# A top-k search and a projection share one stage: four units of projection move from beside the second search to behind it

## The reference, cut to what matters

```
h = rms_norm(x, norm_g[layer])
proj = h @ w_in[layer]
q, k, v, qi, ki, wi, z_a, u_b, z_b, gates = jnp.split(proj, SPLIT_POINTS, axis=-1)
...
logits = jnp.einsum('bqhd,bsd->bqhs', qib, ki)
iscore = jnp.einsum('bqhs,bqh->bqs', jax.nn.relu(logits), wib).astype(jnp.float32)
iscore = jnp.where(allowed[None], iscore, -jnp.inf)
_, idx = lax.top_k(iscore, k_sel)
...
a = dsa_attention(q, k, v, qi, ki, wi, k_sel) * jax.nn.silu(z_a)
b = multiscale_pool(u_b, pool_w[layer], pool_scale[layer]) * jax.nn.silu(z_b)
g = jax.nn.sigmoid(gates.reshape(B, S, N_BRANCHES, D_MODEL) + merge_bias[layer])
```

## Time and profile before

| | |
|---|---|
| median of 3 runs | 3318.81 us (3316.91 to 3326.31) |
| profiled execution | 3323.57 us, span of its trace 3321.8 us |
| TensorE busy | 3110.3 us (94%) |
| DVE, ACT, POOL busy | 1732.5, 1552.3, 956.3 us |
| second search (32 tries) | 808 to 988 us of the span |
| masks of the second batch, then the barrier | 988 to 1042 us of the span |

### The profile page before, as it was taken

The page is one execution under the profiler, slowest core; times in us unless marked ns, Lnnn a source line. Parts: engine busy times, 40 slices in busy tenths (PEclk is TensorE's granted clock), DMA queues, the critical chain, the costliest instruction groups (busy, mean ns, idle before and its releaser), DMA issues. The chain is left out here.

```text
span 3321.8 us, 43017 instructions
## 1 busy us (share of the span) xinstructions
PE 3110.3 (94%) x15772; PEld 2529.6 (76%) x15772; DVE 1732.5 (52%) x3657; ACT 1552.3 (47%) x2448; POOL 956.3 (29%) x701
## 2 busy tenths in 40 slices
PE   8995999889995999997999799979999999989998
PEld 7994888768884677765778678868888888868787
DVE  6775799989996665536531166642211231133423
ACT  4544688756983677762111143324444354431111
POOL 3541012200222566642222133312322222212222
PEclk9996999999997999998999899989999999999999
DMA  5656333253334621106552345464344543355422
GB/s 177 206 182 231 96 96 100 80 189 110 100 102 155 198 78 51 39 20 192 155 146 93 131 150 161 140 212 142 114 131 137 197 125 118 119 152 157 133 102 89
DMA packets 431706, 440.63 MB, mean 133 GB/s; under 512 B 31008, under 2 KB 324256, under 8 KB 431392
## 3 DMA queue, kind: packets, MB, share of 16 engines
q1 hardware_dynamic: 431520, 438.18, 42.7%
HBM read 279.51 MB, written 158.60 MB: 132 GB/s over the span
## 5 line engine op out<-in xcount | busy, mean ns | idle before, releaser
L1342 PE MATMUL p_pr<-p_hT,p_w_hi 128*128 128x512 f32 x896 | 354.8, 396 | 16.1 <-POOL p_w_lo L1095 10.0
L1343 PE MATMUL p_pr<-p_hT,p_w_hi 128*128 128x512 f32 x896 | 352.3, 393 | 0.0
L1344 PE MATMUL p_pr<-p_hT,p_w_lo 128*128 128x512 f32 x896 | 352.0, 393 | 0.0
L1628 POOL TENSOR_TENSOR a_prob<-a_prob,a_inv 128x1024 f32<-128x1024 f32 (+12 forms) x104 | 250.7, 2419 | 211.2 <-DVE a_inv L1673 211.0
L1135 ACT ACTIVATE p_relu<-p_isc,p_level 128x2048 int8<-128x2048 f32 (+5 forms) x192 | 276.4, 1441 | 22.5 <-DVE p_level L1232 17.7
L791 PE MATMUL t_pj_ps<-t_w_hi,t_hT_slot 128*128 128x356 f32 (+2 forms) x768 | 272.2, 354 | 11.5 <-DVE t_w_lo L639 5.9
L1095 POOL TENSOR_TENSOR p_w_lo<-p_w_raw,p_w_hi 128x256 fp32r<-128x256 f32 x144 | 107.5, 777 | 603.7 <-DVE p_level L1232 399.6
L793 PE MATMUL t_pj_ps<-t_w_hi,t_hT_slot 128*128 128x356 f32 (+2 forms) x768 | 265.2, 345 | 0.0
L792 PE MATMUL t_pj_ps<-t_w_lo,t_hT_slot 128*128 128x356 f32 (+2 forms) x768 | 264.8, 345 | 0.0
L1648 DVE CUSTOM_DVE_ANT_0 a_prob<-a_s_ps,a_mask 128x512 f32<-128x512 f32 (+3 forms) x320 | 189.4, 607 | 141.2 <-PE a_s_ps L1782 136.5
L2260 PE MATMUL o_b_ps<-o_in_hi,o_w_hi 128*128 128x512 f32 x512 | 209.0, 408 | 39.5 <-DVE o_in_lo L2147 27.4
(11 more groups left out here) (291 smaller groups left out, 7120.4 us busy)
## 6 DMA issues: line engine op xcount, KB each, us to landing
s_hT<-t_hT_slot SPq DMA_DIRECT2D x32, 1024.0 KB, 5.9
s_gT<-p_o_sb SPq DMA_DIRECT2D x128, 256.0 KB, 4.9
o_gates<-s_gT SPq DMA_DIRECT2D x64, 512.0 KB, 5.1
p_w_raw<-in_w_in SPq DMA_DIRECT2D x56, 512.0 KB, 4.3
t2n_w_raw<-in_w_in SPq DMA_DIRECT2D x56, 512.0 KB, 4.2
s_qT<-t_qT_slot SPq DMA_DIRECT2D x32, 512.0 KB, 2.7
p_hT<-s_hT SPq DMA_DIRECT2D x32, 512.0 KB, 9.3
s_zuT<-p_o_sb SPq DMA_DIRECT2D x64, 256.0 KB, 4.8
```

The source lines that it names most:

```text
L1342: nc.tensor.matmul(pr[n % NPR][:], wh, hi, start=(k == 0), stop=False)
L1343: nc.tensor.matmul(pr[n % NPR][:], wh, lo, start=False, stop=False)
L1344: last = nc.tensor.matmul(pr[n % NPR][:], wl, hi, start=False, stop=(k == KD - 1))
L1628: nc.gpsimd.tensor_tensor(p, p, f, ALU.mult).then_inc(normed, 1)
```

## The change

`TRY_UNITS[1]` ends at 102 in place of 106. So thirty units, 72 to 101, stand beside the 32 tries of the second search in place of thirty-four, and ten, 102 to 111, behind it in place of six. Only seven `sides` and mask stores stand there, so the two loops of SP and ACT now run on behind the seventh.

```diff
     IDX_UNITS = [(0, 15), (52, 72)]
-    TRY_UNITS = [(15, 52), (72, 106)]
+    TRY_UNITS = [(15, 52), (72, 102)]
...
             last = TRY_UNITS[1][1]
-            for b in range(-2, NB):
-                if b >= 0:
+            for b in range(-2, N_UNITS - last):
+                if 0 <= b < NB:
                     store_mask(1, b)
                 if last + b + 2 < N_UNITS:
                     unit(last + b + 2)
...
-            for b in range(NB):
-                sides(1, b)
-                if b < N_UNITS - TRY_UNITS[1][1]:
-                    unit(TRY_UNITS[1][1] + b)
+            for b in range(N_UNITS - TRY_UNITS[1][1]):
+                if b < NB:
+                    sides(1, b)
+                unit(TRY_UNITS[1][1] + b)
```

## The result

| | before | after |
|---|---|---|
| median of 8 runs | 3322.23 us (3316.91 to 3328.23) | 3332.18 us (3325.77 to 3336.07) |
| profiled execution, its span | 3323.57, 3321.8 us | 3336.07, 3334.3 us |

The ratio is 1.0029, 95% interval 1.0018 to 1.0040: 9.6 us slower, 6 to 13 us by the interval. The two profiled executions are 12.5 us apart, and this stage accounts for most of that. It is measured from DVE's first count of the second search to the next stage's first load, since the search began 0.93 us later in the new trace: 1042.23 - 808.57 = 233.66 us before, and 1053.78 - 809.50 = 244.28 us after, 10.6 us more.

What follows compares the result with a forecast made beforehand. DVE's chain was taken to set the search and masks to end the stage; after the change TensorE's late last units end it, next load at 1053.8 against 1042.23: +11.6 us on 3318.81 gives 3330.4 us, range 3323 to 3336.

Steps and rivals of the forecast that it cites:

- search, to the last level: Second search on DVE: no try has two units, so the store wait at try 15 goes, -2.5 us.
- settling: DVE's small steps behind the search's last level, carried over unchanged at 7.4 us.
- fifth signs: ACT's signs behind the search, waiting for DVE's third mask to be combined; due at 1016.2.
- rest of chunk 55: POOL's w_lo of the last chunk, beside DVE's fourth mask: begun at 1018.7, ready at 1024.6.
- unit 108: TensorE behind the search: starts at 1024.6 after 7 us idle, takes 7.76 us at a low clock.
- last evacuation to the next stage's first load: Stage end: store issued near 1049.5, landing 3.0 us, then 1.25 us to the next load at 1053.8.
- the split of chunk 55: On ACT behind the search: the deciding step, now behind signs that wait for the third mask.
- POOL's blocks: w_lo parts beside the masks: one meeting a DVE scan or combination ends about 0.6 us after it.
- The price for DVE: Masks behind the search: an estimated 1.2 us for each that meets POOL, one before, three now.
- TensorE's lag in the search: TensorE waits 1.9 us for chunk 46's w_lo, growing to 2.9 us by chunk 52; costs the stage nothing.
- the stall ahead of 106: TensorE behind the search waits for chunk 53's w_lo, from 993.8 to 1004.2, then a low clock.
- SP: Chunk 55's load delays unit stores, so ACT's evacuation of unit 104 waits until 1010.2 at most; cost 0.

Runs made afterwards that it cites:

- e2: Twelve units behind the second search in place of the six of the kernel before: stage 258.09 us, median 3345.89 us, ratio 1.0075.
- e3: Changed kernel, but ACT splits chunk 55 behind unit 104's evacuation, ahead of the fourth signs: stage 235.59 us, median 3323.49 us, ratio to before 1.0008.
- e1: Eight units behind the second search in place of the six of the kernel before: stage 232.99 us, median 3321.52 us, ratio 1.0006.
- e4: Changed kernel, but DVE in place of POOL forms w_lo of chunks 53, 54 and 55: stage 238.42 us, median 3325.30 us, ratio to before 1.0017.
- e6: Kernel before, but one unit per try and three in the last try of the second search: stage 229.75 us, median 3316.88 us, ratio 0.9988.
- e5: e1 with the stores of units 110 and 111 issued ahead of the seventh mask's store: stage 231.11 us, median 3317.31 us, ratio to before 0.9988.

## Why the prediction held

Times are from the first count of the search, so that both traces can be compared.

| step | predicted | found |
|---|---|---|
| search, to the last level | 179.4 - 2.5 = 176.9 | 176.8 |
| settling | 7.4, as before | 6.0 |
| fifth signs begin | 207.6 | 206.3 |
| rest of chunk 55 on POOL | 5.9 | 6.4 |
| rest of chunk 55 ready | 216.0 | 215.1 |
| unit 108 on TensorE | 7.8 | 8.4 |
| last evacuation to the next stage's first load | 5.1 | 4.4 |
| next stage's first load | 245.2 | 244.3 |

**The chain was the right one.** The forecast named the split of chunk 55 as the step that decides; e2 and e3 show this by moving it, later and earlier, and the stage followed by 13.8 and -8.7 us. e1 shows the point from which it decides: with eight units behind, the masks end the stage and the time is that of before.

**POOL's blocks.** The reading of the parts (each that meets a scan or a combination ends about 0.6 us behind it) gave 6.4 and 5.9 us; found were 6.77 and 6.43. The plain 8.26 of the earlier trace rows would have been 1.5 and 1.8 us too long. This fits the lock of the Trainium skill's page "SBUF — State Buffer", section "SBUF: two separate sides"; e4 fits it too: there, with POOL idle, DVE's combination of 1920 columns took 2.22 us, where it took 2.64 beside POOL in the changed kernel. The price for DVE, 1.2 us for each mask that meets POOL, is borne out across runs: from the first count to the last mask's start e6, e5 and the change, with one, two and three such masks, take 226.5, 227.7 and 228.9 us.

**The term that was missed.** The settling got shorter by 1.4 us, because POOL no longer formed chunk 54's rest beside it; I had carried it over unchanged. POOL and DVE over time in the kernel before, then DVE's same step after the change:

```profile
987.95 2.83 POOL L1095 TENSOR_TENSOR p_w_lo<-p_w_raw,p_w_hi 128x256 fp32r<-128x256 f32 x4 [7.87 <-ACT p_w_hi L1105]
...
988.14 0.57 DVE L1245 TENSOR_TENSOR p_prefix<-p_level,p_turned_bits 128x7 int32<-128x7 int32 x1
```
```profile
986.43 0.17 DVE L1245 TENSOR_TENSOR p_prefix<-p_level,p_turned_bits 128x7 int32<-128x7 int32 x1
```

A smaller term was also too long: the tail from the last evacuation to the next load took 4.4 us and not 5.1, as the last four unit stores landed in 2.4 us (their median) and not 3.0. Against these two stand POOL's last block (0.5 us longer than forecast) and unit 108 (0.6 us longer), so the stage was forecast to lose 11.6 us and lost 10.6.

**TensorE's lag in the search.** The wait ahead of unit 92 was forecast at 1.9 us and was 1.93. That the clock would fall behind so short a wait was not: it was at 0.50 in the stretch behind it (the last section has the row). Unit 105 ended 0.9 us later than forecast, and chunk 53's rest came 1.5 us earlier, with the settling; so the stall ahead of 106 was 8.0 us and not 10.4. This moved nothing at the end, as TensorE stood another 6.91 us ahead of unit 108.

**SP.** The evacuation of unit 104 did wait for the store of unit 100, until 1009.04 (forecast: at most 1010.2), and the signs behind it were not delayed, as they then waited 1.48 us for DVE.

**The size of the whole.** +11.6 us forecast, +9.95 by the medians and +9.6 by the ratio. The traced stage gives 10.6: the settling and the tail, less the two terms that ran longer, explain the excess over it, and what is left to the medians is less than their scatter. The forecast time, 3330.4 us, stood on a median of three runs, 3318.81, where eight runs give 3322.23. The measured 3332.18 us lies 1.8 us above it; on the median of eight the same sum would have given 3333.8, which is 1.6 us too much. The base was 3.4 us too low, more than the 1.0 us by which the sum missed the stage, so the difference is the better measure of the prediction.

## What to carry to other kernels

Where work is moved behind a chain of waits in a hand-written order, follow each producer that moves with it, not the work itself: here ten units cost 10 us and eight cost none, because one weight split had slid from behind the third signs to behind the fifth, past two more waits for DVE. Such a producer can be put where its own inputs allow (e3) in place of where its consumer happens to stand. And what ends a stage may be the order of the last stores alone, worth 2 us here (e5).

## What the runs showed of the hardware

A TensorE wait of 1.93 us at 917.55 was followed by the granted clock's lower level in the changed kernel; in e3 a wait of the same 1.93 us at the same place was not, nor in e4 one of 1.89 us. Busy times by stretch, of the changed kernel, of e3 and of e4 (columns as in the earlier trace rows; the seventh figure, behind POOL's, is the clock):

```profile
918.50:920.50 2.00, 2.00 (x6) 1.61 (x5) 1.86 (x8) 1.44 (x4) 0.00 (x0) 0.50 0.82 158
```
```profile
917.00:922.00 5.00, 4.11 (x18) 3.42 (x19) 4.86 (x10) 4.44 (x7) 0.84 (x2) 1.00 0.57 148
```
```profile
917.00:922.00 5.00, 4.82 (x21) 3.98 (x22) 4.86 (x12) 4.44 (x8) 0.12 (x1) 1.00 0.71 200
```

So a wait of this size may or may not cost the clock; what decides between the two, these runs don't show. Four POOL subtractions of 128x256, 2.84 us beside DVE's counts, took 8.25, 6.77, 6.43 and (e2) 4.61 us beside its scans and combinations. And DVE's three small steps of the settling, on 7 or 14 columns, took 0.57 to 0.66 us each in place of 0.17 while POOL ran.
